# Expert stage of a hybrid decoder block: order of ScalarE's work and layout of the weight pieces

## The reference, cut to what matters

```python
# 32 experts (4 groups of 8), every row goes to 2 of them, D_MODEL = 1024, D_EXPERT = 512
def expert_block(args):
    tok, e = args
    xb = x_pad[tok]                              # the expert's rows, gathered
    hb = jax.nn.silu(xb @ w1[e]) * (xb @ w3[e])  # gate and up: 1024 -> 512
    return hb @ w2[e]                            # down: 512 -> 1024
...
out = jnp.zeros((T + 1, D), xn.dtype).at[slot_tok].add(y * slot_w[:, None])[:T]
```

## Time and profile before

| what | value |
|---|---|
| median of three runs | 1956.92 us |
| the profiled execution | 1964.04 us |
| its span | 1962.5 us |
| TensorE, TensorE's weight load | 1738.7 us (89%), 1375.7 us (70%) |
| VectorE, ScalarE, GpSimd | 1042.5 us (53%), 846.8 us (43%), 128.9 us (7%) |
| high parts L1464, 192 of them | 364.6 us, 1916 ns each |
| low parts L1470, 192 of them | 439.5 us, 2291 ns each |

### The profile page before, as it was taken

The page is one execution under the profiler, slowest core; times in us unless marked ns, Lnnn a source line. Parts: engine busy times, 40 slices in busy tenths (PEclk is TensorE's granted clock), DMA queues, the critical chain, the costliest instruction groups (busy, mean ns, idle before and its releaser), DMA issues. The chain is left out here.

```text
span 1962.5 us, 23223 instructions
## 1 busy us (share of the span) xinstructions
PE 1738.7 (89%) x8639; PEld 1375.7 (70%) x8639; DVE 1042.5 (53%) x1123; ACT 846.8 (43%) x862; POOL 128.9 (7%) x170
## 2 busy tenths in 40 slices
PE   4999999999999999988869898569999999999980
PEld 3788888879977878767758798346666666666650
DVE  4343434342205013277764421468888888888866
ACT  5243434331212121155541202237777777777751
POOL 2100000000000000011110000010000000000005
PEclk9999999999999999999999999869999999999995
DMA  5722222222332232644433310859999999999927
GB/s 175 196 94 89 92 90 91 80 90 104 129 118 75 85 110 99 229 152 172 171 111 128 128 55 28 290 195 368 380 376 374 380 376 379 375 375 380 379 83 267
DMA packets 196202, 385.96 MB, mean 197 GB/s; under 512 B 11440, under 2 KB 70904, under 8 KB 192064
## 3 DMA queue, kind: packets, MB, share of 16 engines
q1 hardware_dynamic: 184064, 343.16, 48.9%
q0 software_dynamic: 8384, 29.63, 5.3%
q10 hardware_dynamic: 3712, 12.62, 1.7%
HBM read 317.95 MB, written 67.42 MB: 196 GB/s over the span
## 5 line engine op out<-in xcount | busy, mean ns | idle before, releaser
L1470 DVE TENSOR_TENSOR e_l<-e_raw,e_h 128x2048 fp32r<-128x2048 f32 x192 | 439.5, 2291 | 107.8 <-ACT e_h L1464 105.8
L1464 ACT ACTIVATE e_h<-e_raw 128x2048 fp32r<-128x2048 f32 x192 | 364.6, 1916 | 75.4 <-PE ps L1486 49.4
L193 PE MATMUL ps<-uh,w_h 128*128 128x512 f32 x1024 | 318.2, 392 | 21.5 <-DVE ul L834 13.6
L193 PE MATMUL ps<-ul,w_h 128*128 128x512 f32 x1024 | 317.1, 391 | 0.0
L193 PE MATMUL ps<-uh,w_l 128*128 128x512 f32 x1024 | 316.6, 391 | 0.0
L177 DVE TENSOR_TENSOR w_l<-w_raw,w_h 128x2048 fp32r<-128x2048 f32 x40 | 91.6, 2291 | 361.9 <-ACT w_h L173 361.9
L193 PEld LDWEIGHTS ps<-uh,w_h 128*128 128x128 f32 x1024 | 192.9, 189 | 63.6 <-issue 22.4
L1486 PE MATMUL ps<-e_h,e_xth 128*96 128x512 f32 x512 | 204.9, 400 | 27.3 <-DVE e_l L1470 25.4
L193 PEld LDWEIGHTS ps<-ul,w_h 128*128 128x128 f32 x1024 | 193.4, 189 | 40.6
L193 PEld LDWEIGHTS ps<-uh,w_l 128*128 128x128 f32 x1024 | 193.2, 189 | 40.5
L1486 PE MATMUL ps<-e_h,e_xtl 128*96 128x512 f32 x512 | 202.7, 396 | 0.0
(11 more groups left out here) (246 smaller groups left out, 2167.7 us busy)
## 6 DMA issues: line engine op xcount, KB each, us to landing
e_raw<-w_exp_gate SPq DMA_DIRECT2D x64, 1024.0 KB, 8.6
e_raw<-w_exp_up SPq DMA_DIRECT2D x64, 1024.0 KB, 10.0
e_raw<-w_exp_down SPq DMA_DIRECT2D x64, 1024.0 KB, 10.1
w_raw<-w_in SPq DMA_DIRECT2D x28, 1024.0 KB, 5.5
qk_d<-qk SPq DMA_DIRECT2D x16, 1024.0 KB, 4.1
at_qk<-qk_d SPq DMA_DIRECT2D x8, 2048.0 KB, 8.8
y_d<-e_y ACTq DMA_DIRECT2D x32, 384.0 KB, 6.4
y_d<-zeros POOLq DMA_DIRECT2D x22, 384.0 KB, 11.0
```

Source lines behind the costliest of these rows:

```text
L193: mm = pe.matmul(ps[:, h * HALF:(h + 1) * HALF], w[:, k, :], u[:, k, h * HALF:(h + 1) * HALF], start=first, stop=last)
L1464: act.activation(self.e_h[m % SPLIT][:, :, :], self.e_raw[slot][:, :, :], ACT.Copy).then_inc(self.e_hi[m % SPLIT], 1)
L1470: dve.tensor_tensor(self.e_l[slot][:, :, :], self.e_raw[slot][:, :, :], self.e_h[m % SPLIT][:, :, :].bitcast(F32), ALU.subtract).then_inc( ...
```

## The change

Two things are changed together.

1. ScalarE's order. `rows_out` of expert j-1 (the copy from PSUM) now stands behind the high part of piece 4 of expert j, and its store is a function of its own, `rows_store`, behind silu. Silu stands behind the high part of piece 5.
2. The layout of the pieces. A partition now gets runs of 4 KB. For gate and up two consecutive rows of the matrix go to one partition (RUN = 2), so that chunk k holds the rows 256 (k // 2) + 2 p + k % 2; the transposes of the gathered rows take the columns of x in the same way, every second column (`lanes_of`). A piece of down is now a half of the contraction with all 1024 columns (DOWN_RUN = 1), and `down_products` writes both halves of the result in each piece: the stationary tile stays for two matmuls, and the sum over the contraction goes on over both pieces.

```diff
+RUN, DOWN_RUN = 2, 1
...
-        w = self.ins["w_exp_" + kind][0][e].rearrange("(k p) n -> p k n", p=P)
-        src = w[:, :, half * HALF:(half + 1) * HALF] if kind == "down" else w[:, 4 * half:4 * half + 4, :]
+        run = DOWN_RUN if kind == "down" else RUN
+        lanes = self.ins["w_exp_" + kind][0][e].rearrange("(k p r) n -> p k (r n)", p=P, r=run)
+        n = lanes.shape[1] // 2
         slot, _ = self.raw_slot(piece)
-        eng.dma_start(self.e_raw[slot][:, :, :], src).then_inc(self.e_in[slot], 16)
+        eng.dma_start(self.e_raw[slot][:, :, :].rearrange("p (k r) n -> p k (r n)", k=n), lanes[:, n * half:n * half + n, :])\
+            .then_inc(self.e_in[slot], 16)
+
+    def lanes_of(self, row, chunk, run):
+
+        k, r = chunk // run, chunk % run
+        return row[:, k * P * run:(k + 1) * P * run].rearrange("t (p r) -> t r p", r=run)[:, r, :]
...
+    def down_products(self, pe, ps, ht_h, ht_l, piece, half):
...
+        for k in range(2):
+            at = 2 * half + k
+            for x, w, first, last in ((ht_h, w_h, at == 0, False), (ht_h, w_l, False, False), (ht_l, w_h, False, at == 3)):
+                for c in range(2):
+                    mm = pe.matmul(ps[:, c * HALF:(c + 1) * HALF], x[:, at, :], w[:, 2 * k + c, :], start=first, stop=last)
+        mm.then_inc(self.e_used[m % SPLIT], 1)
...
-                mm = pe.transpose(ps_x[:, k, :], xg[b][:, k * P:(k + 1) * P], ident)
+                mm = pe.transpose(ps_x[:, k, :], k_.lanes_of(xg[b][:, :], k, RUN), ident)
...
-            k_.piece_products(pe, ps_y[:, half * HALF:(half + 1) * HALF], ht_h, ht_l, piece, True, True)
+            k_.down_products(pe, ps_y, ht_h, ht_l, piece, half)
...
             act.activation(y_sb[b][:, :], ps_y[:, :], ACT.Copy).then_inc(y_out, 1)
+
+        def rows_store(act, j, b):
             act.wait_ge(y_out, j + 1)
...
                 def body(j, b, first=False, last=False):
                     k_.piece_hi(act, (j, b, 4))
+                    if not first:
+                        rows_out(act, j - 1, 1 - b, (j, b, 1))
+                    k_.piece_hi(act, (j, b, 5))
                     act_silu(act, j, (j, b, -1) if not first else (0, 0, 1))
-                    for m in (5, 6):
-                        k_.piece_hi(act, (j, b, m))
+                    if not first:
+                        rows_store(act, j - 1, 1 - b)
+                    k_.piece_hi(act, (j, b, 6))
...
                         x_high(act, j + 2, b, (j, b, 3))
-                    rows_out(act, j, b, (j, b, 7))
```

More of the change, by code:

```diff
@@ L1486, in piece_products @@
                 mm = pe.matmul(ps, x[:, k, :], w[:, k, :], start=first and first_piece, stop=last and last_piece)
+        mm.then_inc(self.e_used[m % SPLIT], 1)
+    def down_products(self, pe, ps, ht_h, ht_l, piece, half):
+        j, b, m = piece
+        slot, _ = self.raw_slot(piece)
+        pe.wait_ge(self.e_lo[m % SPLIT], 2 * j + m // SPLIT + 1)
+        w_h, w_l = self.e_h[m % SPLIT], self.e_l[slot]
+        for k in range(2):
[3 more added lines that the diff above has]
+                    mm = pe.matmul(ps[:, c * HALF:(c + 1) * HALF], x[:, at, :], w[:, 2 * k + c, :], start=first, stop=last)
         mm.then_inc(self.e_used[m % SPLIT], 1)
@@ L1711, in _ @@
                 j, b = NE - 1, 1
+                k_.piece_hi(act, (j, b, 4))
+                rows_out(act, j - 1, 0, (j, b, 1))
                 act_silu(act, j, (j, b, -1))
-                for m in (4, 5):
-                    k_.piece_hi(act, (j, b, m))
+                rows_store(act, j - 1, 0)
+                k_.piece_hi(act, (j, b, 5))
                 h_high(act, j, (j, b, 1))
                 rows_out(act, j, 1, (j, b, 5))
+                rows_store(act, j, 1)
                 def other(j, b, t):
@@ L1727, in other @@
                     rows_out(act, j, b, (j, b, 5))
+                    rows_store(act, j, b)
                 beyond(act, other)
```

## The result

The changed kernel's median is 1935.27 us (four runs, 1933.35 to 1942.25), beside 1956.65 us for the kernel before (1956.08 to 1962.54): a ratio of 0.9885, 95% interval 0.9855 to 0.9916. It is faster, by 16 to 28 us, and inside the range of 1918 to 1944. The forecast was 1928, so 7 us of the gain are missing. In a later set of runs the changed kernel had a median of 1934.98 us beside 1961.82 us, ratio 0.9862, interval 0.9835 to 0.9889.

The account below looks back on a forecast made before the run. TensorE with its gap was taken to bound the expert stage, the DMA engines just as fast. 1964.0 - 31.5 (gap) + 2.1 (silu wait) = 1934.6 us profiled; 7.1 us off for the median gives 1928 us, range 1918 to 1944.

Parts of the forecast that it names:

- The gap and who ends it: Expert stage: TensorE idles 1.08 us an expert until VectorE's low part of piece 4, held up by ScalarE's late high part.
- What is late next: ScalarE's new row up to silu: gate's piece 4 starts slightly late behind silu, charged 0.07 us an expert.
- the second rival: Behind the copy: gate waits for silu; half the gain gone, 1942 us, chance 0.10, or no change, 1957 us, 0.05.
- Two limits side by side: Expert stage: TensorE with its gap and the DMA engines both need 18.80 us an expert; a change must move both.
- The stock: Weight pieces in the expert stage: each lands 17.1 us before its use, covering a shortfall of 0.5 us an expert.
- rival 1: Expert loads get no faster; TensorE uses up 17.1 us of early-landed data, then 18.8 us an expert; 1940 us, chance 0.14.
- The loads at 4 KB: Expert weight loads: six pieces at 413 GB/s in place of 387, 1.03 us less, so 17.77 us an expert.
- The stepped transposes: Eight row transposes an expert: stepped stationary loads cost between 0 and 1.63 us more; nothing taken.
- The third rival: Row transposes: stepped loads take twice as long, unhidden, 1.63 us more an expert; slower, 1976 us, chance 0.05.
- Paired products: Down's 24 matmuls, paired on one stationary tile: 0.1 us an expert at best, 0 taken.
- The sum: Whole kernel: 1964.0 - 31.5 + 2.1 = 1934.6 us for the profiled execution.
- From the profiled execution to the median: Whole kernel: the profiled run stood 7.1 us over the median of 1956.92, so the median after is 1927.5 us.

Follow-up runs that it names:

- `e2_layout_only`: The changed kernel with ScalarE's order of the kernel before, so only the new layout; 1966.94 us beside 1961.91 for the kernel before, ratio 1.0030.
- `e1_order_only`: The kernel before with only ScalarE's new order, keeping 2 KB runs and unstepped transposes; 1936.46 us beside 1961.91 for the kernel before, ratio 0.9870.
- `e9_store_with_copy`: The changed kernel with result copy, its wait, store and silu all between the high parts of pieces 4 and 5; 1957.92 us, ratio 0.9980 to the kernel before.
- `e10_copy_behind_5`: The changed kernel with the result copy moved behind the high part of piece 5, silu after it; 1966.24 us, ratio 1.0015 to the kernel before.
- `e3_packed_turn`: The changed kernel with transposes reading 128 columns in a row, rows and weights mismatched in gate and up; 1930.16 us, ratio 0.9838 to the kernel before.
- `e6_norm_lanes`: The changed kernel with VectorE's norm writing columns in lane order, so transposes need no step; 1924.11 us, ratio 0.9812 to the kernel before.

## Why the prediction was right, and where it was not

- **The gap and who ends it.** Right. 1.08 us an expert, owed to the copy, its wait and the store ahead of the high part; `e2_layout_only` keeps the gap with the order, `e1_order_only` and the changed kernel lose it.
- **What is late next.** Right, and narrow. I had silu end 0.07 us ahead of its use, took 0.15 us for TensorE to start behind it, and charged 0.07 us an expert; it ends 0.1 us ahead and nothing is late. Of what I called 0.1 us to spare in two places, `e9_store_with_copy` and `e10_copy_behind_5` show what it is worth: another order in that row brings 0.7 to 0.9 us an expert back. So the second rival (a part of the gap comes back behind the copy) didn't happen, but its condition was close.
- **Two limits side by side.** Right for the pace, not for what I drew from it, that a change must move both. With 2 KB runs the loads need 18.67 us an expert, against the 18.80 that I took as a bound. The stock covers 17 experts, which is why the order alone comes out at the same time as both parts (1936.46 us, and 1940 in rival 1).
- **The loads at 4 KB.** The direction was right, the size too good: I took 17.77 us from a stretch of 6 us with one kind of transfer (413 GB/s); with the gather and the store beside them, the loads need 17.95 us. They gain 0.72 us an expert and not 1.03; how much of the rest is the gather and the store, and how much the shortness of that stretch, is not shown. The changed kernel, at 17.96 us, doesn't feel it, and without the step the stock of 17 us hides it: 0.28 us an expert over the stage is some 9 us.
- **The stepped transposes: the step that failed.** "I take nothing, since the nearest row is the same load without the step." That row could not say anything about the step. Measured are 0.26 us an expert in the transposes and 0.29 us in the pace, within my bounds of 0 and 1.63. The third rival named the right place and even too small a load, 200 ns for the measured 221; its price was 0.26 and not the 1.01 us from which it decides, since it took the loads for unhidden, and they overlap (a transpose every 0.109 us). The rule of the Trainium skill ("SBUF — State Buffer", Door 1: The DMA port swizzle, the note on cachelines) that two hits on a 16-byte line keep full rate doesn't hold for this load: with two hits it takes 221 ns, with one hit 218 ns, and in a row 140 ns. The measurement decides.
- **Paired products.** Nothing taken, nothing found: the second piece of down takes 1503.28 - 1500.43 = 2.85 us, and 1516.00 - 1513.14 = 2.86 us before.
- **The sum, and luck in it.** Silu's first and last of 32 starts are 578.6 us apart before (1313.9 to 1892.5), 553.8 in the changed kernel (1310.6 to 1864.4) and 545.4 in `e3_packed_turn` (1308.4 to 1853.8). So without the step the stage would have gained 33.2 us, 3.8 more than the 29.4 of my sum, and the step takes 8.4 back. What is left, 24.8 us, is 4.6 less than I forecast. The medians of the first comparison show 21.4 us, since three of the four runs of the kernel before were near 1956 us; in the later one (1961.82 and 1934.98) they show 26.8. The missing 7 us are thus 4.6 us of the stage and, for the rest, as far as is known, the spread of the kernel before.
- **From the profiled execution to the median.** I took 7.1 us off, since the profile of before stood that much over its median. Of the kernel before some runs are at 1956 and some at 1962 to 1967, and the profiled one was of the latter. In the two profiled executions a part of the difference lies ahead of the experts: the first norm before routing starts at 1230.3 us before and at 1224.1 in the changed kernel. The same stretch of the mixer, before and after:

```profile
840.00:975.00 135.00, 115.15 (x605) 94.58 (x605) 97.55 (x293) 68.96 (x168) 21.07 (x45) 0.92 0.49 175
```

```profile
840.00:975.00 135.00, 115.27 (x648) 95.41 (x648) 104.33 (x312) 73.59 (x179) 22.50 (x48) 0.97 0.49 175
```

  The granted clock of TensorE is 0.92 of full speed there in the one and 0.97 in the other, with 605 and 648 matmuls in it. It is so in all twelve traces: the seven with 0.97 or 0.98 there start that norm at 1222.3 to 1224.7 us, the five with 0.92 or 0.94 at 1226.7 to 1231.1. Why the clock differs there is not shown. The spans differ by 30.1 us (1962.5 and 1932.4), and 6.2 of these lie ahead of that norm and have nothing to do with the change. That the profiled execution came out at 1933.84 us, beside a forecast of 1934.6 for it, is luck: these 6.2 us stand in for what the stage didn't gain. A comparison of single runs of this kernel is good to some 7 us only.

## What to carry to other kernels

Two engines that are both full don't say which of them a change must speed up: the stock of landed data and the time from issue to landing say it, together with how long the issues themselves take, and a change that frees one limit shows the other only when the stock is gone, so look at the pace early and late in a stage. When an instruction is moved ahead on a busy engine, lay out the whole row up to the next thing that someone waits for; two of three orders with the same first step kept 0.4 and 0.2 of 1.1 us here. And a layout that makes one access contiguous makes another one stepped: pay for the step once, where it is cheap, as `e6_norm_lanes` does.

## What the runs showed of the hardware

- A stationary load of TensorE, 96 x 128 float32, takes 140 ns in a row, 221 ns at a step of two values and 218 ns at a step of four. Beside a stream of transposes, their distance goes from 0.076 us (0.61 / 8) to 0.109 us (0.87 / 8), each time about half of what one load takes, so the loads overlap.
- VectorE's multiply of 1024 float32 takes 1282 ns in a row and 2072 ns when both inputs have a step of eight values; 512 values at a step of two take 747 ns.
- Where the loads fell behind, which shows what they can do in this mix, the DMA engines moved 378 to 382 GB/s with 2 KB runs (`e1_order_only`, share 1.04 to 1.05) and 394 to 397 GB/s with 4 KB runs (`e3_packed_turn`, 1350 to 1750 us, share 1.03). The share doesn't tell who waits: it was 1.04 at 377 GB/s in the kernel before and 1.01 at 372 GB/s in `e2_layout_only`, where the gap of TensorE set the pace.
